# Function tables of the scalar engine, loaded by one-element activations placed ahead of waits

## The chip, the core and the metric

The kernel runs on one core of a Trainium2 chip. A core has five engines that run their own instruction streams and meet at semaphores: TensorE (matmul; PE in the profile, PEld its weight loads), VectorE (DVE), ScalarE (ACT), GpSimd (POOL) and SyncE (SP). Sixteen DMA engines move data between the device memory and the core's two on-chip memories. The metric is the device time of one execution in microseconds.

ScalarE computes functions such as Exp, Sqrt, Sigmoid, Silu and GELU from tables. The tables come in sets; an instruction ACT_TABLE_LOAD in its stream puts another set in place. The programmer doesn't write these loads: they are inserted into the program where an activation needs a table that isn't in place. Copy, Identity, Square and Relu need no set of their own.

## The reference, cut to what matters

A token block of 256 x 1024 goes through three parts. Part one (one layer):

```python
mod = silu(c) @ w_ada + b_ada                      # nine rows of modulation
h = modulate(rmsnorm(x), m0, m1); y = swiglu(h)    # ffn 1
x = x + 0.5 * m2 * rmsnorm(y)
h = modulate(rmsnorm(x), m3, m4)                   # sparse attention beside an LRU
x = x + m5 * rmsnorm(concat(rmsnorm(attn), rmsnorm(lru)) @ w_out)
h = modulate(rmsnorm(x), m6, m7); y = swiglu(h)    # ffn 2
x = x + 0.5 * m8 * rmsnorm(y)
```

Parts two and three are two layers of a second block. Each has a mixer (HGRN2, dilated attention and Mamba2 side by side, between two RMS norms) and a layer of picked experts: 8 heads pick 16 experts per token each, and for each pick `x += gelu(h . down[e]) * gate * up[e]`.

## The kernel before, in words

**Part one** goes stage by stage through both 128-token blocks. On ScalarE each RMS norm is a `mean_square`: a Square over the row with an accumulated sum, a wait for it, and a Sqrt of one element per partition. It is called by `pre` (norm of x, after a wait for `x_ready`), `post` (norm of a product in PSUM, after a wait for `tiles_used`) and `attn_norm` (after a wait for `attn_scaled`). The feed-forward gates are Silu (L1314, in `ffn`).

**Parts two and three** run over four units i = 0 to 3: two layers by two token blocks. Each has a mixer (`mixer_scalar`, `mixer_vector`, `mixer_tensor`) and then its picks (`picks_scalar`, `picks_vector`, `picks_tensor`, `picks_pool`). Mixer 0 runs alone (`lone`). Mixers 1 to 3 run beside the picks of the unit before: a mixer is a generator that yields a slot number ahead of each of its steps, and `Beside.to(slot)` runs all steps up to that slot. The picks of a unit are 8 heads x 8 rounds = 64 rounds of two picks; on ScalarE and VectorE round r calls `beside.to(2 * r + 1)`, so slots go up to 127, and on TensorE each of the 128 picks calls `beside.to(k)`. The order of the work on each engine is so written out by hand.

One round of picks: POOL gathers a pick's row of 2 x 1024 values (down and up) for each of 128 tokens (L1158), into a ring of 8 buffers; VectorE takes the dot product with h (L1107); ScalarE takes the GELU of two dots (L1021); VectorE multiplies by the gate (L1118); ScalarE scales the identity to two diagonal matrices (L1026); TensorE adds diagonal x up row into PSUM (L1040). POOL gathers into a buffer again when TensorE has used it (`ups_used`). VectorE waits for the GELU of a round before it goes on to the next round's dots.

Once a head, `exps(u + 1)` takes the exponentials of the next head's scores (L1007), at the start of a head; for the head that begins the next unit it is taken in the last head's third round. `opening` runs ahead of the first round of all: `post(2, 1)`, the last norm of part one, for the second token block.

The mixer's steps on ScalarE that need tables, with their slots: L316 Sqrt (1), L327 Sigmoid (13), L342 and L343 Exp (28), L362, L363 and L385 to L387 Silu (42; 50 for L362 and L363 when not lone), L396 Sqrt (46), L378 Sqrt (46 lone, else 55), L419 and L422 Exp (57), L429 Exp in `probs` (62 and 67), L367 Silu (55 lone, else 68), L446 Sqrt (69), L464 Sqrt (91). Steps that only copy lie between them.

The weights come over SP's queue in tiles of 1 MB into a ring of four buffers; TensorE frees one with `tiles_used`. The second feed-forward's down product of the second token block (L1753, "late" tiles) is spread through mixer 0 on TensorE and ends just ahead of `opening`.

Of the kernel before, what the change touches and what calls it, by code (L numbers as in the profile page):

```python
# [6 lines left out]


# [1 line left out]

# [1 line left out]

# [8 lines left out]
ACT = mybir.ActivationFunctionType  # L21
AX = mybir.AxisListType

P = 128
# [26 lines left out]
EXPERT_HEADS = 8  # L51
# [6 lines left out]
ROUNDS = K16 // ROUND  # L58
# [35 lines left out]
def columns(spec):  # L94

    at, out = 0, {}
    for name, n in spec:
        out[name] = at
        at += n
    return out, at  # L100
# [8 lines left out]
CONST = [("ident", P), ("eps", 1), ("iota", K16), ("ones", P), ("tri", P), ("trineg", P), ("hmask", 7 * P)]  # L109
EARLY = P + 1 + K16  # L110
WAVE = 3
CONST1 = [("t5", BANK), ("dil", BANK), ("chunk", TB * S)]
CC1, WC1 = columns(CONST1)
CC, WC = columns(CONST)


def program(nc, wts, ada, c_row, small1, small2, consts, consts1, x_in, lb_in, normrow, experts, out):
    ctx = ExitStack()
    with ctx:
        def sb(name, shape, dt=F32, stack=ctx):  # L120
            return stack.enter_context(nc.sbuf_tensor(name, shape, dt))

        def sem(name):
            return ctx.enter_context(nc.semaphore(name))
# [6 lines left out]
        bias_d1 = sb("bias_d1", [P, A2, S])  # L131
        stat = sb("stat", [P, 64])
        mst = sb("mst", [P, 72])
        s2 = sb("s2", [P, LAYERS, W2])
        lbt = sb("lbt", [P, 8])
        PS = ctx.enter_context(nc.psum_tensor("PS", [P, 8, BANK], F32))
# [26 lines left out]
        m = {n: sem(n) for n in names}  # L163
# [91 lines left out]
        def o1(name, a=0, n=1, rows=P):  # L255
            return s1[0:rows, C1[name] + a:C1[name] + a + n]
# [21 lines left out]
        class Count:  # L278
# [4 lines left out]
            def next(self):  # L283
                self.n += 1
                return self.n

        class Beside:
# [3 lines left out]
                self.at = next(steps, None)  # L291

            def to(self, slot):
                while self.at is not None and self.at <= slot:
                    self.at = next(self.steps, None)

        def mixer_scalar(act, i):
            lone = i == 0
# [5 lines left out]
                return PS[:, c % 2, :]  # L304

            yield 1
            if i >= TB:
                act.wait_ge(m["x_added"], i - TB + 1)
            else:
                act.wait_ge(m["x_ready"], 5 + i)  # L310
                act.wait_ge(m["smalls2_loaded"], 32)
# [53 lines left out]
            def chunk6():  # L365
                a = chunk(6)
                act.activation(u[:, 640:768], a[:, 0:128], ACT.Silu)  # L367
                act.copy(v_tok[:, tb, :], a[:, 128:512]).then_inc(m["u_copied"], 1)

            def o_squares():  # L370
                act.wait_ge(m["o_done"], i + 1)
                for h in range(4):
                    act.activation(osq[:, h * DH:(h + 1) * DH], PS[:, 1, h * DH:(h + 1) * DH], ACT.Square,
                                   accum_out=mst[:, 28 + h:29 + h]).then_inc(m["o_sq"], 1)

            def o_root():
                act.wait_ge(m["o_sq"], 4 * i + 4)
                act.activation(mst[:, 32:36], mst[:, 28:32], ACT.Sqrt, bias=C("eps"), scale=1.0 / DH).then_inc(m["o_root"], 1)  # L378
# [12 lines left out]
                act.copy(Wx.rearrange("p (b n) -> p b n", b=2), PS[:, G2:G2 + 2, 0:256]).then_inc(m["cross_copied"], 1)  # L391
            yield 46
            if lone:
                o_squares()
            act.wait_ge(m["qk_sums"], i + 1)
            act.activation(mst[:, 16:28], mst[:, 4:16], ACT.Sqrt, bias=C("eps"), scale=1.0 / DH).then_inc(m["qk_root"], 1)  # L396
# [17 lines left out]
            else:  # L414
                o_squares()
                o_root()
            yield 57
            act.wait_ge(m["cum_in"], i + 1)
            act.activation(dts[:, 78:90], dts[:, 66:78], ACT.Exp).then_inc(m["cum_exp"], 1)  # L419
            act.wait_ge(m["cum_T"], i + 1)  # L420
# [17 lines left out]
            if not lone:  # L438
                chunk6()
            yield 69  # L440
            act.wait_ge(m["y_gated"], i + 1)
            for g in range(2):
                act.activation(Wx[:, 192 * g:192 * g + 192], mx[:, 640 + 192 * g:832 + 192 * g], ACT.Square,
# [10 lines left out]
            for b in (0, 1):  # L454
# [3 lines left out]
                                          scale=o2(l, "mix_g", c))  # L458
                last.then_inc(m["hT_mix"], 1)
            yield 91  # L460
            act.wait_ge(m["x_out"], i + 1)
            act.activation(flat(lgt)[:, 0:D], x[:, tb, :], ACT.Square, accum_out=mst[:, 2:3]).then_inc(m["out_sq"], 1)
            act.wait_ge(m["out_sq"], i + 1)
# [539 lines left out]
        def picks_scalar(act, i, beside=None, opening=None):  # L1003

            def exps(u):
                act.wait_ge(m["topk_ready"], u + 1)
                act.activation(topf[:, 128 + 32 * (u % 2):144 + 32 * (u % 2)], topf[:, 112 + 32 * (u % 2):128 + 32 * (u % 2)],  # L1007
                               ACT.Exp).then_inc(m["gate_exp"], 1)

            if i == 0:  # L1010
                exps(0)
            for h in range(EXPERT_HEADS):
                u = EXPERT_HEADS * i + h
                if h + 1 < EXPERT_HEADS:
                    exps(u + 1)
                if u == 0:
                    opening()
                for rr in range(ROUNDS):
                    rnd = u * ROUNDS + rr
                    act.wait_ge(m["dots_done"], rnd * ROUND + ROUND)  # L1020
                    act.activation(coef[:, 0, rr % 2, :], dots[:, rr % 2, :], ACT.Gelu_apprx_tanh).then_inc(m["gelu_ready"], 1)  # L1021
                    act.wait_ge(m["coef_ready"], rnd + 1)
                    if rnd * ROUND >= RING:
                        act.wait_ge(m["ups_used"], rnd * ROUND + ROUND - RING)
                    for j in range(ROUND):
                        act.activation(diag[:, (rr * ROUND + j) % RING, :], ident, ACT.Copy, scale=coef[:, 1, rr % 2, j:j + 1])\  # L1026
                            .then_inc(m["diag_ready"], 1)
                    if beside:
                        beside.to(2 * (h * ROUNDS + rr) + 1)
                        if h + 1 == EXPERT_HEADS and rr == 2:  # L1030
                            exps(u + 1)

        def picks_tensor(pe, i, beside=None):
            if i:
                pe.wait_ge(m["x_added"], i)
            for k in range(PICKS):
                n = PICKS * i + k
                pe.wait_ge(m["diag_ready"], n + 1)
                for half in range(2):
                    last = pe.matmul(PS[:, ACC + half, :], diag[:, n % RING, :], ups[:, n % RING, half * BANK:(half + 1) * BANK],  # L1040
                                     start=k == 0, stop=k == PICKS - 1, skip_group_check=True)
                last.then_inc(m["ups_used"], 1)
                if beside:
                    beside.to(k)
# [142 lines left out]
        def _(sp):  # L1187
            for n in range(TILES):
# [4 lines left out]
                elif n == 2:  # L1193
                    sp.wait_ge(tile_loaded[0], 16)
                elif n == WAVE:
                    sp.wait_ge(m["mod_added"], 14)
# [37 lines left out]
        def _(act):  # L1234
# [7 lines left out]

            def pre(k, tb):
                if k:
                    act.wait_ge(m["x_ready"], 2 * (k - 1) + tb + 1)
                mean_square(x[:, tb, :], D, 4 * k + 2 * tb, D, "x_root")

            def post(i, tb, done, bank):
                act.wait_ge(m["tiles_used"], done)
                mean_square(flat(PS[:, bank:bank + 2, :]), D, 12 + 4 * i + 2 * tb, D, "y_root_fb",  # L1250
                            flat(lgt) if i == 2 and tb else junk)
# [16 lines left out]
            act.dma_start(cst[:, 0:EARLY], consts[:, 0:EARLY]).then_inc(m["consts_loaded"], 16)  # L1268
            act.dma_start(s1[:, :], small1).then_inc(m["smalls_loaded"], 16)
            act.dma_start(cst1[0:33, 0:2 * BANK], consts1[0:33, 0:2 * BANK]).then_inc(m["strip_loaded"], 16)  # L1270
            act.wait_ge(m["c_spread"], 1)
            act.activation(cact[:, :], flat(PS[:, 0:2, :]), ACT.Silu).then_inc(m["c_act"], 1)
            act.wait_ge(m["x_loaded"], 16)
            act.wait_ge(m["consts_loaded"], 16)
            for tb in range(TB):
                pre(0, tb)
# [139 lines left out]
                act.copy(dst, flat(PS[:, bank:bank + 2, :])).then_inc(m["probs_copied"], 1)  # L1416

            def attn_norm(tb):
                act.wait_ge(m["attn_scaled"], tb + 1)
                mean_square(attn[:, tb, :], D_ATTN, 24 + 2 * tb, D_ATTN, "attn_root")  # L1420

            def attn_evacuate(tb):
                act.wait_ge(m["attn_T"], tb + 1)
                for c in range(4):
                    last = act.activation(mT[:, c, tb * P:(tb + 1) * P], PS[:, 4 + tb, c * P:(c + 1) * P], ACT.Copy,
                                          scale=o1("attn_g", c))
                last.then_inc(m["attn_by_scalar"], 1)
# [16 lines left out]
            act.activation(scr1[:, 2048:3072], scr1[:, 0:1024], ACT.Square).then_inc(m["lru_sq"], 1)  # L1444
            attn_norm(1)
            attn_evacuate(1)
            act.wait_ge(m["lru_sumsq"], 1)
            act.activation(lroot, PS[:, 6, 0:S], ACT.Sqrt, bias=C("eps"), scale=1.0 / D_ATTN)\
                .then_inc(m["lru_root"], 1)
# [15 lines left out]
        def _(pe):  # L1465
# [60 lines left out]
            def gate_up(f):  # L1526
# [8 lines left out]

                for j in range(0 if f else WAVE, 4):
                    step(j, 0, True)
# [38 lines left out]
            for c in range(3, KC):  # L1576
                for j in range(WAVE):
                    wave(j, c, c + 1)
# [202 lines left out]
        def _(v):  # L1781
            V = Chain(v, m["chain_v"])
# [67 lines left out]
            def pair_columns(c):  # L1850
# [3 lines left out]
                v.scalar_tensor_tensor(prea[:, c:c + 1], modc[:, 8 + c:9 + c], 1.0, o1("pre_g", c), ALU.add, ALU.mult)\  # L1854
                    .then_inc(m["first_cols"], 1)

            v.memset(silu[0:1, 0, 0:P], 1.0).then_inc(m["c_ones"], 1)
            v.wait_ge(m["c_act"], 1)
            pair_sums(0)
# [289 lines left out]
```

## Time and profile before

| | us |
|---|---|
| Median of three runs | 2228.6 (2226.3 to 2235.58) |
| The profiled execution, whole | 2231.29 |
| Its span in the profile | 2229.6 |
| TensorE busy | 1983.0 (89%) |
| VectorE busy | 1293.3 (58%) |
| ScalarE busy | 631.8 (28%) |
| GpSimd busy | 610.2 (27%) |

The profile shows one execution. The span counts from its first to its last instruction; the execution lasts 1.7 us longer. A line such as L1021 is that line of the kernel. Registers, branches and the issue of DMAs do not count as busy. The mean granted clock of TensorE is 0.97 of full speed. A group of instructions has the idle time of its engine just before them, and what ended most of it. The chain that ended last is followed back from the last instruction to what released it.

### The profile page before, as it was taken

What the parts mean: (1) busy time and instruction counts of PE and PEld (TensorE: products, weight loads), DVE (VectorE), ACT (ScalarE), POOL (GpSimd) and SP (SyncE); (2) the same over time, 40 slices, a digit from 0 to 9 for tenths busy, and PEclk for the clock granted to TensorE, in tenths of its full rate; (3) what the DMA queues carried; (4) which work ended last, traced back from release to release, by engine and by line L of the source; (5) the groups of instructions that cost most, each with busy time, mean ns of one, the idle gap of its engine ahead of it and who ended that gap; (6) DMA issues with size and microseconds to landing.
All of it is one profiled execution on the core that took longest, in us unless ns stands there. A gap on an engine that the chain in (4) does not pass through costs nothing.

```text
span 2229.6 us, 20053 instructions
## 1 busy us (share of the span) xinstructions
PE 1983.0 (89%) x6132; PEld 1065.8 (48%) x6132; DVE 1293.3 (58%) x3375; ACT 631.8 (28%) x1517; POOL 610.2 (27%) x554
## 2 busy tenths in 40 slices
PE   7999999899999898888879998998989899777776
PEld 5885587588644344443434443443434444333322
DVE  5550254200033567786576877657687767777764
ACT  2000234200024222543142255223235422222221
POOL 1100000000000233443343333334334334454442
PEclk9999999999999999999999999999999999899999
DMA  9988834444676899999999999999999999999997
GB/s 394 421 351 310 313 114 150 170 151 151 243 266 222 323 420 421 413 419 400 421 413 421 421 420 402 403 422 412 421 406 410 391 420 406 399 421 422 421 421 320
DMA packets 113382, 793.89 MB, mean 356 GB/s; under 512 B 12378, under 2 KB 16090, under 8 KB 18442
## 3 DMA queue, kind: packets, MB, share of 16 engines
q0 software_dynamic: 78912, 574.65, 62.5%
q1 hardware_dynamic: 28944, 207.73, 24.7%
q10 hardware_dynamic: 5434, 10.41, 1.3%
q8 instruction: 42, 0.69, 0.1%
q14 instruction: 50, 0.41, 0.0%
HBM read 791.67 MB, written 4.75 MB: 357 GB/s over the span
## 4 chain that ended last, share of the span: by engine, by line
PE 54%; DMA 22%; DVE 12%; ACT 7%; issue 4%; POOL 1%; POOLq 0%; DVEq 0%; ACTq 0%
DMA wide<-experts_in,pick_idx 20%; PE PS L1474 16%; PE PS L1040 16%; PE PS L496 9%; PE PS L1548 6%; DVE wide L1107 4%; ACT diag L1026 2%; PE PS L1753 1%; ACT L1021 1%; POOL wide L1158 1%; DMA ring<-wts_in 1%; DMA early<-ada_in 1%; PE PS L1505 1%; DVE topi L1055 1%; DVE topi L1058 1%
## 5 line engine op out<-in xcount | busy, mean ns | idle before, releaser
L1040 PE MATMUL PS<-wide,diag 128*128 128x512 f32 x2048 | 988.6, 621 | 206.4 <-ACT diag L1026 197.1
L1158 POOL DMA_INDIRECT wide<-experts_in,pick_idx x512 | 582.8, 1138 | 1286.8 <-PE PS L1040 793.1
L1107 DVE CUSTOM_DVE_ANT_0 wide<-wide,htok 128x1024 f32<-128x1024 f32 x512 | 619.2, 1224 | 242.1 <-DMA wide<-experts_in,pick_idx 235.0
L1040 PEld LDWEIGHTS PS<-wide,diag 128*128 128x128 f32 x2048 | 386.5, 197 | 727.1 <-issue 419.7
L1474 PE MATMUL PS<-hT,ring 128*128 128x256 f32 x1648 | 360.4, 381 | 4.5 <-ACT hT L1257 1.9
L1474 PEld LDWEIGHTS PS<-hT,ring 128*128 128x128 f32 x1648 | 313.9, 191 | 50.5 <-issue 5.8
L496 PE MATMUL PS<-ring,hTm 128*128 128x512 f32 (+1 forms) x704 | 321.8, 586 | 1.9 <-ACT hTm L321 0.8
L1026 ACT ACTIVATE diag<-cst,coef 128x128 f32<-128x128 f32 x512 | 177.6, 394 | 271.9 <-DVE coef L1118 266.7
L1021 ACT ACTIVATE coef<-dots 128x2 f32<-128x2 f32 x256 | 52.1, 204 | 590.5 <-DVE dots L1107 589.9
L496 PEld LDWEIGHTS PS<-ring,hTm 128*128 128x128 f32 x704 | 133.0, 191 | 161.5 <-issue 153.2
L1548 PE MATMUL PS<-ring,actT 128*128 128x512 f32 x264 | 116.1, 600 | 2.4 <-DMA ring<-wts_in 2.4
L1818 DVE TENSOR_TENSOR actT<-silu,PS 128x256 f32<-128x256 f32 (+1 forms) x44 | 18.5, 420 | 170.5 <-ACT silu L1314 170.5
L1314 ACT ACTIVATE silu<-PS 128x256 f32<-128x256 f32 x44 | 16.9, 384 | 271.9 <-PE PS L1474 269.7
L1118 DVE TENSOR_TENSOR coef<-coef,gate 128x2 f32<-128x2 f32 x256 | 41.3, 161 | 87.1 <-ACT coef L1021 74.5
L1811 DVE CUSTOM_DVE_ANT_0 early<-early,cact 128x1024 f32<-128x1024 f32 x56 | 67.0, 1222 | 42.7 <-DMA early<-ada_in 42.7
L1548 PEld LDWEIGHTS PS<-ring,actT 128*128 128x128 f32 x264 | 50.4, 192 | 65.4 <-issue 61.4
L1021 ACT ACT_TABLE_LOAD x61 | 78.3, 1283 | 1.1
L1793 DVE RECIPROCAL stat<-stat 128x1 f32<-128x1 f32 x6 | 1.0, 164 | 111.9 <-ACT stat L1240 111.9
L1228 POOL TENSOR_TENSOR bias_t<-bias_t,early 128x1024 f32<-128x1024 f32 (+1 forms) x2 | 7.9, 3932 | 187.4 <-DVE early L1925 187.4
L1221 POOL DMA_DIRECT2D early<-ada_in x32 | 17.0, 530 | 107.6 <-DVE modr L1811 89.7
L1107 DVE DVE_READ_ACCUMULATOR2_ANT dots<- 128x1 f32 x512 | 42.1, 82 | 0.0
L1753 PE MATMUL PS<-ring,actT 128*128 128x512 f32 x88 | 38.9, 594 | 0.0
(337 smaller groups left out, 1363.4 us busy)
## 6 DMA issues: line engine op xcount, KB each, us to landing
ring<-wts_in SPq DMA_DIRECT2D x191, 1024.0 KB, 5.7
early<-ada_in POOLq DMA_DIRECT2D x36, 1024.0 KB, 12.8
wide<-experts_in,pick_idx POOLq DMA_INDIRECT x512, 11.8
ring<-wts_in SPq DMA_DIRECT2D x8, 780.0 KB, 8.5
strip_t<-strips_one ACTq DMA_DIRECT2D x1, 2048.0 KB, 11.5
strip_dil<-strips_one ACTq DMA_DIRECT2D x1, 1536.0 KB, 19.5
x<-x_in ACTq DMA_DIRECT2D x1, 1024.0 KB, 5.5
bias_t<-strip_t ACTq DMA_DIRECT2D x1, 1024.0 KB, 14.3
```

Of the source, the lines that this page charges most:

```text
L496: last = pe.matmul(PS[:, c % 2, 0:n], hTm[:, k, :], w[:, k % 4 * n:(k % 4 + 1) * n], start=k == 0, stop=k == 7, skip_group_check=True)
L1021: act.activation(coef[:, 0, rr % 2, :], dots[:, rr % 2, :], ACT.Gelu_apprx_tanh).then_inc(m["gelu_ready"], 1)
L1026: act.activation(diag[:, (rr * ROUND + j) % RING, :], ident, ACT.Copy, scale=coef[:, 1, rr % 2, j:j + 1])\
L1040: last = pe.matmul(PS[:, ACC + half, :], diag[:, n % RING, :], ups[:, n % RING, half * BANK:(half + 1) * BANK], start=k == 0, stop=k == PI ...
L1055: V(v.max_index(where[:, 0:8], vals[:, 0:8], row))
L1107: v.tensor_tensor_reduce(out=downs[:, n % RING, :], in0=downs[:, n % RING, :], in1=htok[:, tb, :], scale=1.0, scalar=0.0, op0=ALU.mult, op ...
L1118: v.tensor_tensor(coef[:, 1, rr % 2, :], coef[:, 0, rr % 2, :], gate[:, u % 4, rr * ROUND:(rr + 1) * ROUND], ALU.mult)\
L1158: pool.indirect_dma_start(pairs_of_rows[:, k % RING, :, :].rearrange("p c n -> p (c n)"), None, experts.rearrange("l e d -> (l e) d"), bas ...
L1474: last = pe.matmul(outp, a, b, start=i == 0, stop=i == len(pairs) - 1)
L1548: last = pe.matmul(PS[:, bank + half, :], src[:, 2 * t + k, tb * P:(tb + 1) * P], w[:, k * D + half * BANK:k * D + (half + 1) * BANK], sta ...
L1753: last = pe.matmul(PS[:, 6 + half, :], actT[:, 2 * t + k, P:S], w[:, k * D + half * BANK:k * D + (half + 1) * BANK], start=t == k == 0, st ...
L1811: v.tensor_tensor_reduce(out=w, in0=w, in1=cact[:, :], scale=1.0, scalar=0.0, op0=ALU.mult, op1=ALU.add, accum_out=modr[:, 8 * j + n:8 * j ...
```

## The change

A helper `warm(act, func)` issues a one-element activation (per partition) of a function, from a column of ones to one of 100 columns that nobody reads. Calls of it stand ahead of the waits of ScalarE's norms, of some steps of mixer 0, and in the picks: at the start of each head and at the end of each round in which a mixer step ran. `Beside.to` now says whether a step ran. A memset on VectorE at the very start writes the ones.

```diff
+        warmed = sb("warmed", [P, 1 + WARMED])
             def to(self, slot):
+                ran = False
                 while self.at is not None and self.at <= slot:
                     self.at = next(self.steps, None)
+                    ran = True
+                return ran
+
+        warm_at = itertools.count()
+
+        def warm(act, func):
+            c = next(warm_at) % WARMED + 1
+            act.activation(warmed[:, c:c + 1], warmed[:, 0:1], func)
...
 # mixer_scalar, each after its yield and ahead of the waits
             yield 1
+            if lone:
+                warm(act, ACT.Sqrt)
...
             yield 46
             if lone:
+                warm(act, ACT.Sqrt)
                 o_squares()
...
             yield 57
+            if lone:
+                warm(act, ACT.Exp)
...
             yield 69
+            if lone:
+                warm(act, ACT.Sqrt)
...
             yield 91
+            if lone:
+                warm(act, ACT.Sqrt)
...
 # picks_scalar
             if i == 0:
+                warm(act, ACT.Exp)
                 exps(0)
             for h in range(EXPERT_HEADS):
                 u = EXPERT_HEADS * i + h
                 if h + 1 < EXPERT_HEADS:
                     exps(u + 1)
                 if u == 0:
                     opening()
+                warm(act, ACT.Gelu_apprx_tanh)
                 for rr in range(ROUNDS):
...
                     if beside:
-                        beside.to(2 * (h * ROUNDS + rr) + 1)
+                        ran = beside.to(2 * (h * ROUNDS + rr) + 1)
                         if h + 1 == EXPERT_HEADS and rr == 2:
                             exps(u + 1)
+                        if ran or h + 1 == EXPERT_HEADS and rr == 2:
+                            warm(act, ACT.Gelu_apprx_tanh)
...
             def pre(k, tb):
                 if k:
+                    warm(act, ACT.Sqrt)
                     act.wait_ge(m["x_ready"], 2 * (k - 1) + tb + 1)
...
             def post(i, tb, done, bank):
+                warm(act, ACT.Sqrt)
                 act.wait_ge(m["tiles_used"], done)
...
+            act.wait_ge(m["c_ones"], 1)
             act.wait_ge(m["c_spread"], 1)
             act.activation(cact[:, :], flat(PS[:, 0:2, :]), ACT.Silu).then_inc(m["c_act"], 1)
+            warm(act, ACT.Sqrt)
             act.wait_ge(m["x_loaded"], 16)
...
             def attn_norm(tb):
+                warm(act, ACT.Sqrt)
                 act.wait_ge(m["attn_scaled"], tb + 1)
...
             attn_evacuate(1)
+            warm(act, ACT.Sqrt)
             act.wait_ge(m["lru_sumsq"], 1)
...
+            V(v.memset(warmed[:, 0:1], 1.0))
             v.memset(silu[0:1, 0, 0:P], 1.0).then_inc(m["c_ones"], 1)
```

## Rows read from the trace of the kernel before

**Rows 1.** The page, part 4: shares of the chain that ended last, by line.

```profile
DMA wide<-experts_in,pick_idx 20%; PE PS L1474 16%; PE PS L1040 16%; PE PS L496 9%; PE PS L1548 6%; DVE wide L1107 4%; ACT diag L1026 2%; PE PS L1753 1%; ACT L1021 1%; POOL wide L1158 1%; DMA ring<-wts_in 1%; DMA early<-ada_in 1%; PE PS L1505 1%; DVE topi L1055 1%; DVE topi L1058 1%
```

**Rows 2.** The page, part 5: groups; busy us, mean ns, idle before, releaser.

```profile
L1021 ACT ACTIVATE coef<-dots 128x2 f32<-128x2 f32 x256 | 52.1, 204 | 590.5 <-DVE dots L1107 589.9
...
L1021 ACT ACT_TABLE_LOAD x61 | 78.3, 1283 | 1.1
```

**Rows 3.** Timeline of ScalarE: start us, us, what, [idle before, releaser].

```profile
424.74 1.28 ACT L1314 ACT_TABLE_LOAD   x1
433.46 0.38 ACT L1314 ACTIVATE silu<-PS 128x256 f32<-128x256 f32 x1 [7.44 <-PE PS L1474]
```

**Rows 4.** The chain in order of time: start us, us, what; at the start and at 616.

```profile
9.35 12.54 DMA early<-ada_in
...
616.23 10.30 PE PS L1753 x24
```

**Rows 5.** Timeline of ScalarE, the square of attn_norm(0).

```profile
372.33 0.63 ACT L1238 ACTIVATE silu<-early 128x512 f32<-128x512 f32 x1 [0.33 <-DVE early L1965]
```

**Rows 6.** Timeline of all engines, 695 to 699, mixer 0.

```profile
695.77 0.36 ACT L443 ACTIVATE Wx<-mx 128x192 f32<-128x192 f32 x1 [1.52 <-DVE mx L978]
...
696.13 1.88 PE L1753 MATMUL PS<-ring,actT 128*128 128x512 f32 x4
...
698.71 1.10 PE L683 MATMUL PS<-v_tok,hTm 128*128 128x64 f32 x8 [0.69 <-ACT hTm L449]
```

**Rows 7.** Timeline at the opening; last, a stage: window, us, engines, PEclk, DMA share, GB/s.

```profile
760.30 1.02 ACT L1238 ACTIVATE lgt<-PS 128x1024 f32<-128x1024 f32 x1 [6.09 <-PE PS L1753]
...
761.43 1.28 ACT L1240 ACT_TABLE_LOAD   x1
...
762.73 0.29 ACT L1240 ACTIVATE stat<-stat,cst 128x1 f32<-128x1 f32 x1
...
763.05 0.16 DVE L1793 RECIPROCAL stat<-stat 128x1 f32<-128x1 f32 x1 [2.02 <-ACT stat L1240]
...
764.00:766.00 2.00, 0.00 (x0) 0.00 (x0) 1.93 (x4) 0.53 (x2) 0.50 (x1) 0.50 0.98 414
```

**Rows 8.** Timeline of ScalarE, two small activations in a row.

```profile
652.37 0.21 ACT L342 ACTIVATE dts<-s 128x6 f32<-128x6 f32 x1 [0.92 <-DVE dts L869]
652.48 0.19 ACT L343 ACTIVATE dts<-dts 128x6 f32<-128x6 f32 x1
```

**Rows 9.** Waits: who waited for whom, us in total, times, longest.

```profile
DVE coef L1118 <- ACT coef L1021: 74.5, 65, 5.7
```

**Rows 10.** Timeline of ScalarE around slot 47 and slot 63 of unit 0.

```profile
917.07 1.28 ACT L1007 ACT_TABLE_LOAD   x1
...
918.60 1.28 ACT L1021 ACT_TABLE_LOAD   x1
...
960.20 1.28 ACT L429 ACT_TABLE_LOAD   x1
...
963.48 0.20 ACT L1007 ACTIVATE topf<-topf 128x16 f32<-128x16 f32 x1
963.69 1.28 ACT L1021 ACT_TABLE_LOAD   x1
```

**Rows 11.** Stages of 20 us; the last two columns are DMA share and GB/s.

```profile
1000.00:1020.00 20.00, 15.42 (x38) 6.74 (x38) 14.68 (x36) 8.31 (x23) 6.44 (x7) 0.91 0.95 378
...
1760.00:1780.00 20.00, 14.50 (x37) 6.45 (x36) 15.20 (x37) 8.43 (x23) 7.41 (x7) 0.91 0.90 358
```

**Rows 12.** Timeline of GpSimd and VectorE: issues of two gathers and their dots.

```profile
993.89 1.03 POOL L1158 DMA_INDIRECT wide<-experts_in,pick_idx  x1 [2.56 <-PE PS L1040]
...
1003.75 1.23 DVE L1107 CUSTOM_DVE_ANT_0 wide<-wide,htok 128x1024 f32<-128x1024 f32 x1 [0.77 <-DMA wide<-experts_in,pick_idx]
...
1012.37 1.05 POOL L1158 DMA_INDIRECT wide<-experts_in,pick_idx  x1 [6.31 <-PE PS L1040]
...
1018.64 1.23 DVE L1107 CUSTOM_DVE_ANT_0 wide<-wide,htok 128x1024 f32<-128x1024 f32 x1 [1.18 <-DMA wide<-experts_in,pick_idx]
```

More of the change, by code:

```diff
@@ L9 @@
 from contextlib import ExitStack
+import itertools
 import numpy as np
@@ L111 @@
 WAVE = 3
+WARMED = 100
 CONST1 = [("t5", BANK), ("dil", BANK), ("chunk", TB * S)]
```

## The prediction

> **What bounds the kernel now.** I read the page's shares of the chain that ended last first, then ScalarE's groups by line, then the table loads one by one along ScalarE's timeline. By line the chain is gather DMAs (20%) and TensorE matmuls; ScalarE's lines have 2% and 1% [rows 1]. So ScalarE, though it stands in every link, is seldom what is late. The second view decides what the change can do: 61 table loads in front of the GELU of L1021 take 78.3 us, and the idle time ahead of all 61 is 1.1 us, while the GELUs behind them idle 590.5 us waiting for dot products [rows 2]. A load is therefore run as soon as ScalarE reaches it, ahead of the wait of the activation that needs it. A single case shows the same: the load of L1314 starts at 424.74, its activation at 433.46 after 7.44 us of waiting for TensorE [rows 3]. Wherever an activation with one wait is itself the one that needs the table, the load is already where the change wants it. What the change can move are the loads that stand between a sum of squares (which needs no table of its own) and the root after it: there the wait is ahead of the squares, and the load behind them.
>
> The stages: up to about 745 us the kernel is bound by weight DMAs and then by TensorE; from 750 on the gathers saturate the DMA engines (share 0.98 to 1.05 in nearly every slice), with one dip in each of the three token blocks that have a mixer beside them: 0.95 in the slice at 1000, 0.90 in that at 1760, the third between them [rows 11].
>
> **What the change removes: loads from behind squares.** Each is one load of 1.28 us [rows 2]; what follows is whether anything was late because of it.
> - Start (L1240, pre(0, 0)): the chain there is two transfers of the modulation weights until 9.35 + 12.54 = 21.89 [rows 4], long behind ScalarE's root. Gain 0. The new memset ahead of c_ones and the wait for it lie beside the same transfers: 0.
> - post(0, 0) at 224 and post(2, 0) at 616: TensorE carries the chain through with other tiles, in the second case L1753, 10.30 us without a pause [rows 4]. Gain 0.
> - attn_norm(0), attn_norm(1): the idle time before the squares is 0.33 us in the first [rows 5] and none in the second, so the load only changes places with them. 0.33 less about 0.11 for the extra activation, then the same in loss: 0.
> - Mixer 0, L396 at 681: TensorE has tiles of L496 to work on meanwhile and goes on to its next turn without a pause. Gain 0.
> - Mixer 0, L446 at 696.59: on the chain, L443 to the load to L449 to L683. Ahead of L443 ScalarE idles 1.52 us, which just covers the load (1.28) and an activation. But TensorE is on L1753 until 696.13 + 1.88 = 698.01 and starts L683 at 698.71 [rows 6]: when the load goes, L1753 is late next. Gain 698.71 - 698.01 = 0.7 us, not 1.28.
> - The opening of the picks, post(2, 1): square at 760.30 after 6.09 us idle, load at 761.43, and VectorE starts on its root at 763.05 [rows 7]. VectorE, the first weights and the first diagonals come 1.28 earlier. The DMA engines are at share 0.98 in the slice that follows [rows 7], so the freed buffers join a full queue. Between 0 and 1.28; I take 0.6, since the queue is full but the first re-issue comes late (POOL waits there).
> Sum: -1.3 us (bounds -2.0 and -0.7).
>
> **What it adds: activations.** Counting the code: 119 in the picks (one for each of 32 heads, one after each of 28 rounds in which a mixer step ran, one more in the last head, the last two in three blocks), and some 20 elsewhere that lie in waits. Behind another ready activation, a small one costs the spacing of L342 and L343, 0.11 us; at most its length of 0.19 [rows 8]. It costs nothing where ScalarE then waits for dot products. It counts where VectorE waits for the GELU, which the waits give 65 times [rows 9]: 65 x 0.11 = 7.2 us (upper bound 65 x 0.19 = 12.4).
>
> **What it adds: table loads.** This is the part that the words of the change do not mention. The diff puts a GELU activation at the end of every round in which a mixer step ran. In the last round of a head the next thing on ScalarE is not a GELU but the exponential of L1007. Two mixer steps with other tables fall on such rounds, at slots 47 and 63 of the 128:
> - Slot 47: L396 (root), then L1007's load at 917.07, then L1021's at 918.60 [rows 10]. With a GELU between L396 and L1007 there is one load more.
> - Slot 63: L429 (exponential) with its load at 960.20, then L1007 at 963.48 with none, as the table is there, then L1021's load at 963.69 [rows 10]. With a GELU between them, both a GELU load and an exponential load are added: two more.
> Three loads in each of three blocks: 9 x 1.283 = 11.5 us of ScalarE, always where VectorE sits waiting for the GELU. The Trainium skill, ScalarE: Activation LUTs, Rules for kernel authors, says to group calls by table set and to finish one set before switching; slot 63 is where the old code does so and the new code does not. By that rule the sum is the one just made.
>
> The waits that are added (c_ones) are met long before ScalarE comes there. Of the queues, none is passed: the activations stand ahead of waits and behind issued DMAs. Queued behind each extra load are the GELU, the two diagonals, TensorE's products and then POOL's next gather.
>
> **How much of it reaches the end.** ScalarE's extra time is 11.5 + 7.2 = 18.7 us, 6.2 in each of three blocks. A gather that is issued later need not land later as long as the DMA queue holds others. The gather of the pick dotted at 1003.75 was issued at 993.89, 9.9 us before; the one dotted at 1018.64 was issued at 1012.37, 6.3 us before, with the DMA engines just run dry [rows 12]. The difference, 3.6 us, is an estimate of what the queue can swallow ahead of the dip. So a block is longer by 6.2 - 3.6 = 2.6 us, three by 7.8 us. Bounds: 0, if a faster stretch behind the mixer's rounds gives it all back, and 18.7 if nothing is swallowed.
>
> Sum: -1.3 + 7.8 = +6.5 us. The profiled execution took 2231.3 (span 2229.6 and 1.7 around it) and would take 2237.8; the median of the runs is 2228.6, 2.7 lower, so I forecast 2228.6 + 6.5 = 2235 us.
>
> **Rivals.**
> 1. Nothing is swallowed. Between 910 and 990 VectorE hardly waits for gathers; the chain there runs through ScalarE and VectorE, and a longer link is then longer 1:1. For it: DMA share still dips in each block, so the ring of eight rows is empty once per block [rows 11]. Against it: the share is 1.01 throughout the very stretch in which the loads are added. Time 2228.6 - 1.3 + 18.7 = 2246.0. It decides once the added delay exceeds those 3.6 us by much in a single stretch. 21%.
> 2. All is swallowed, or the compiler adds no loads at the two slots. Only the gains show: 2228.6 - 2.0 = 2226.6, to 2228. For it: from 750 on bytes over rate set the pace. 23%.
> 3. The loads do not now run ahead of the waits, and the change takes the 61 off the chain: up to 61 x 1.28 = 78 us less, 2150. Against it: 1.1 us of idle time ahead of 61 loads [rows 2]. 1%. Some gain of over 11 us from elsewhere, for which I have no row: 3%.
> 4. A switch costs more than its load, up to twice as much. Then the nine cost 9 x 2 x 1.283 = 23.1 us, and the time is 2228.6 - 1.3 + 23.1 + 7.2 - 3 x 3.6 = 2246.8. Against it: the load ends at 761.43 + 1.28 = 762.71 and its activation starts at 762.73 [rows 7], so 1.28 is all. 3%. The Trainium skill, ScalarE: Activation LUTs, What ACT_TABLE_LOAD costs, does put a drain of about 1.38 us on every switch, 2.66 in all; the rows do not agree.
>
> **How the numbers follow.** Likeliest case 49%, 2231 to 2241 by the bounds of its terms; rivals 21, 23, 4 and 3%. The range 2226 to 2246 holds the likeliest, most of rival 2 and the lower part of rival 1. A measurement of this kernel tells about 0.5%, 11 us, from no change: slower is above 2239.7, faster below 2217.5. Slower: rivals 1 and 4 and an upper slice of the likeliest, 0.27. Faster: 0.04. Within: 0.69.
>
> **What would show it.** In ScalarE's groups, L1007's and L1021's loads, with those of the new activations, up by 9 from 89, and 6 loads of L1240 (now moved to the new line) no longer behind squares. At slot 63, four loads where two stood. The idle time of VectorE before L1118 up by 10 to 18 us. The first diagonal about 2 us earlier. DMA shares at the three dips lower by 0.1 each if the likeliest holds, unchanged in rival 2. I am wrong in the main step if the number of loads is not up, or if it is and the dips have not moved.

## The result and the profile after

| | before | changed |
|---|---|---|
| Median, us | 2228.6 (2224.02 to 2235.58, 7 runs) | 2244.49 (2239.87 to 2251.61, 7 runs) |
| Ratio | | 1.0076, 95% interval 1.0063 to 1.0088 |
| Span of the profiled execution, us | 2229.6 | 2247.4 |
| ScalarE busy, us | 631.8 | 658.9 |
| Mean granted clock of TensorE | 0.97 | 0.96 |

The changed kernel is slower: by 15.9 us between the medians, by 0.76% (17 us) in the ratio. The median is 1.5 us below the upper end of the stated range and 4.8 us above the 2239.7 us from which the forecast calls it slower. It is near the time of the first rival (2246) and 9.5 us above the likeliest case (2235).

In the changed kernel L308 is the new activation, L1029 is the old L1007 (exponentials of a head), L1045 the old L1021 (GELU), L1050 the old L1026 (diagonals), L1066 the old L1040, L1133 the old L1107 (dots), L1144 the old L1118, L1184 the old L1158 (gathers), L447 the old L429, L463 the old L443, L705 the old L683, L1785 the old L1753. Its groups, with busy us, mean ns and idle time before, answer [rows 2]:

```profile
L1045 ACT ACTIVATE coef<-dots 128x2 f32<-128x2 f32 x256 | 51.2, 200 | 569.9 <-DVE dots L1133 569.7
...
L308 ACT ACT_TABLE_LOAD x77 | 98.8, 1283 | 1.4
...
L1029 ACT ACT_TABLE_LOAD x30 | 38.5, 1283 | 0.4
L308 ACT ACTIVATE warmed<-warmed 128x1 f32<-128x1 f32 x139 | 28.1, 204 | 7.2 <-issue 6.4
```

The 61 loads of L1021 have moved to L308, with all the others that were moved; six more are new there, and three new ones stand at L1029, which lost one of its old loads to L308. Summed over all groups the loads went from 150 to 159. As before, a load waits for nothing (1.4 us ahead of 77), and the GELU behind it still idles 570 us.

Where the nine stand, on ScalarE's timeline of the changed kernel: slot 47 of unit 0 and slot 63 of unit 2. They answer [rows 10]:

```profile
919.55 1.28 ACT L308 ACT_TABLE_LOAD   x1
920.84 0.20 ACT L308 ACTIVATE warmed<-warmed 128x1 f32<-128x1 f32 x1
921.05 1.28 ACT L1029 ACT_TABLE_LOAD   x1
...
922.58 1.28 ACT L308 ACT_TABLE_LOAD   x1
...
1731.76 1.28 ACT L447 ACT_TABLE_LOAD   x1
...
1735.14 1.28 ACT L308 ACT_TABLE_LOAD   x1
...
1736.65 1.28 ACT L1029 ACT_TABLE_LOAD   x1
...
1738.17 1.28 ACT L308 ACT_TABLE_LOAD   x1
...
1739.58 0.19 ACT L1045 ACTIVATE coef<-dots 128x2 f32<-128x2 f32 x1
```

At slot 63 four loads stand where two stood: the exponential table is thrown out after 1735.14 and fetched again at 1736.65 for one activation of 0.22 us.

The gains ahead of the picks are there too. Timeline of all engines, mixer 0 (answers [rows 6]) and the opening (answers [rows 7]):

```profile
695.44 0.36 ACT L463 ACTIVATE Wx<-mx 128x192 f32<-128x192 f32 x1
...
695.80 1.88 PE L1785 MATMUL PS<-ring,actT 128*128 128x512 f32 x4
...
697.52 1.00 PE L705 MATMUL PS<-v_tok,hTm 128*128 128x64 f32 x8
...
759.01 1.02 ACT L1264 ACTIVATE lgt<-PS 128x1024 f32<-128x1024 f32 x1 [4.59 <-PE PS L1785]
...
760.48 0.16 DVE L1825 RECIPROCAL stat<-stat 128x1 f32<-128x1 f32 x1 [0.58 <-ACT stat L1266]
```

From the squares to TensorE's next product: 2.08 us, before 2.94, so 0.86 less (forecast 0.7; L1785 is what is late now). From the square of the opening to VectorE: 1.47 us, before 2.75, the one load of 1.28 less. The first diagonals start at 764.69 instead of 767.26, 2.6 us earlier.

### The profile page after: what moved, and what is told of

Read it like the earlier page. It is cut to its first block, busy times and chain, and to the rows that moved or that the text cites. A ratio compares the mean times of both kernels' runs of the same rounds, so it can differ in the third digit from the quotient of the medians.

```text
span 2247.4 us, 20203 instructions
## 1 busy us (share of the span) xinstructions
PE 2007.3 (89%) x6132; PEld 1080.2 (48%) x6132; DVE 1292.3 (58%) x3376; ACT 658.9 (29%) x1665; POOL 616.3 (27%) x554
## 4 chain that ended last, share of the span: by engine, by line
PE 59%; DMA 20%; DVE 9%; ACT 6%; issue 4%; POOL 1%; POOLq 0%; DVEq 0%; ACTq 0%
PE PS L1066 20%; DMA wide<-experts_in,pick_idx 18%; PE PS L1506 16%; PE PS L518 10%; PE PS L1580 6%; DVE wide L1133 3%; PE PS L1785 2%; ACT diag L1050 1%; ACT L308 1%; POOL wide L1184 1%; DMA ring<-wts_in 1%; DMA early<-ada_in 1%; PE PS L512 1%; PE PS L1537 1%; ACT L1029 1%
## 5 line engine op out<-in xcount | busy, mean ns | idle before, releaser
L1066 PE MATMUL PS<-wide,diag 128*128 128x512 f32 x2048 | 1005.1, 631 | 201.3 <-ACT diag L1050 195.2
L1184 POOL DMA_INDIRECT wide<-experts_in,pick_idx x512 | 589.0, 1150 | 1298.7 <-PE PS L1066 804.6
L1133 DVE CUSTOM_DVE_ANT_0 wide<-wide,htok 128x1024 f32<-128x1024 f32 x512 | 618.4, 1223 | 237.1 <-DMA wide<-experts_in,pick_idx 230.3
L1066 PEld LDWEIGHTS PS<-wide,diag 128*128 128x128 f32 x2048 | 393.0, 200 | 725.2 <-issue 429.0
L1050 ACT ACTIVATE diag<-cst,coef 128x128 f32<-128x128 f32 x512 | 177.6, 394 | 274.9 <-DVE coef L1144 274.9
L1045 ACT ACTIVATE coef<-dots 128x2 f32<-128x2 f32 x256 | 51.2, 200 | 569.9 <-DVE dots L1133 569.7
L1144 DVE TENSOR_TENSOR coef<-coef,gate 128x2 f32<-128x2 f32 x256 | 41.1, 161 | 118.9 <-ACT coef L1045 100.6
L1133 DVE DVE_READ_ACCUMULATOR2_ANT dots<- 128x1 f32 x512 | 41.8, 82 | 0.0
L1785 PE MATMUL PS<-ring,actT 128*128 128x512 f32 x88 | 38.9, 594 | 0.0
## 6 DMA issues: line engine op xcount, KB each, us to landing
strip_dil<-strips_one ACTq DMA_DIRECT2D x1, 1536.0 KB, 18.7
```

The lines of the kernel that those rows point to most:

```text
L1133: v.tensor_tensor_reduce(out=downs[:, n % RING, :], in0=downs[:, n % RING, :], in1=htok[:, tb, :], scale=1.0, scalar=0.0, op0=ALU.mult, op ...
L1144: v.tensor_tensor(coef[:, 1, rr % 2, :], coef[:, 0, rr % 2, :], gate[:, u % 4, rr * ROUND:(rr + 1) * ROUND], ALU.mult)\
L1184: pool.indirect_dma_start(pairs_of_rows[:, k % RING, :, :].rearrange("p c n -> p (c n)"), None, experts.rearrange("l e d -> (l e) d"), bas ...
L1785: last = pe.matmul(PS[:, 6 + half, :], actT[:, 2 * t + k, P:S], w[:, k * D + half * BANK:k * D + (half + 1) * BANK], start=t == k == 0, st ...
```

## The experiments

Two theories. L: what costs is the nine table loads at slots 47 and 63, on the chain of ScalarE. A: what costs is the 119 one-element activations. Each kernel was timed in five rounds beside the kernel before on the same chip; the ratios are to that, with 95% intervals.

**1. The nine loads alone.**

```diff
 # the kernel before, in picks_scalar, behind beside.to(...)
+                        if rr + 1 == ROUNDS and h in (2, 3):
+                            warm(act, ACT.Gelu_apprx_tanh)
```

> The kernel before with a GELU activation at the end of the last round of heads 2 and 3 of each unit with a mixer beside it, and nowhere else: 6 activations and the 9 table loads that they bring. Theory L (the loads on ScalarE's chain at slots 47 and 63 are the cost): 9 x 1.28 us reach the end nearly whole, 9 to 14 us over the kernel before, about 2240. Theory A (the 119 activations are the cost): 6 x 0.11, under 1 us over, 2229. My forecast of record (3.6 us of each block swallowed by the DMA queue): 3 x (4.1 - 3.6), under 3 us over.

Measured: 2242.96 us, ratio 1.0055 (1.0041 to 1.0068). The same kernel in a later series on another chip gave 2244.59 us, ratio 1.0050 (1.0032 to 1.0067), expected as

> The nine loads alone once more, on the same chip as the two kernels above: 0.55% again, within 0.14.

That is 11 to 12 us for 9 x 1.283 = 11.5 us of loads. Theory L holds, theory A falls for this part, and so does the forecast's term for what the queue swallows, which left under 3 us.

**2. The activations alone.** The same 119 places, with `ACT.Copy` in place of the GELU, and no front.

> The kernel before with all 119 activations of the picks, as copies, which need no table: activations without loads, and nothing changed ahead of the picks. Theory L: 0 to 4 us over the kernel before. Theory A: 8 to 17 us over.

Measured: 2232.62 us, ratio 1.0008 (0.9998 to 1.0018), 1.8 us. VectorE's wait for the GELU grew nonetheless, from the 74.5 us of [rows 9] to:

```profile
DVE coef L1134 <- ACT coef L1035: 83.0, 66, 5.8
```

8.5 us more of waiting, 7.2 by the forecast's reckoning, but some 2 us of it reach the end (at most 4.0 by the interval).

**3. The changed kernel without the 12 activations at head ends.**

```diff
-                        if ran or h + 1 == EXPERT_HEADS and rr == 2:
+                        if ran and (rr + 1 < ROUNDS or h + 1 == EXPERT_HEADS) or h + 1 == EXPERT_HEADS and rr == 2:
                             warm(act, ACT.Gelu_apprx_tanh)
```

> The changed kernel without the 12 activations that end the last round of a head where a mixer step ran and the next head's exponentials come next. It has the gains ahead of the picks, 107 activations in the picks, and 150 table loads as before. Theory L: -3 to +4 us against the kernel before. Theory A: +8 to +15, nearly as the changed kernel.

Measured: 2230.71 us, ratio 0.9991 (0.9978 to 1.0005). The whole loss is gone with 12 of 139 activations and the nine loads that they brought. The loads are 150 again, and at slot 63 the head's exponential runs on the mixer's table:

```profile
965.55 0.20 ACT L1029 ACTIVATE topf<-topf 128x16 f32<-128x16 f32 x1
965.76 1.28 ACT L308 ACT_TABLE_LOAD   x1
```

**4. The front alone** (no GELU activation in the picks).

> The changed kernel without any GELU activation in the picks: only the loads moved from behind squares, and the exponential at the first head. Both theories: -0.7 to -2.0 us against the kernel before, by the terms of the forecast; the square of post(2, 1) to the first diagonal shorter by one load. If the shift of the picks' start against the weights is itself harmful (a third theory), it is slower, by 2 us or more.

Measured: 2229.58 us, ratio 0.9992 (0.9980 to 1.0003): 1.8 us less, in keeping with the forecast's 1.3, but not told from no change.

**5. The changed kernel again.**

> The changed kernel as it is, beside the next three on one chip. If the parts add up (nine loads +0.55%, the activations +0.08%, the front -0.08%) it is 0.5 to 0.65% slower than before; if they make each other worse, 0.75 to 0.9%.

Measured: 2249.43 us, ratio 1.0082 (1.0068 to 1.0095). That is the second case: all parts together cost more than their sum. Experiment 8 asks which part does it.

**6 and 7. Three of the loads, and the other six.** `h == 2` alone (slot 47), then `h == 3` alone (slot 63).

> The kernel before with the GELU activation only at slot 47 of units 0 to 2: three loads of the nine, one in each block, 1.4 us each. If the queue swallows 3.6 us ahead of each dip, as the forecast has it: 0. If a load on the chain costs its length: 4 to 5 us. If the cost is one of place (a threshold that the two slots pass together): under 2 us here, and the rest at slot 63.

Measured: 2235.41 us, ratio 1.0023 (1.0011 to 1.0035).

> The kernel before with the GELU activation only at slot 63 of units 0 to 2: six loads, two in each block. By the price per load of the three loads at slot 47 (0.23%, 1.7 us each): 10 us, 0.46%. If parts add up to the nine loads' 0.55%: 0.32%, 7 us, 1.2 us a load.

Measured: 2237.89 us, ratio 1.0029 (1.0019 to 1.0039). 5.1 and 6.5 us; together 0.52%, the nine loads' 0.50 to 0.55%. A single load in a block already costs something near its length: 1.7 us each, 0.8 to 2.6 by the interval, against 1.28 and the activation's 0.2. There is no threshold of 3.6 us below which it is free. The six at slot 63 came out at 1.1 us a load, so a second load at one place was not seen to be dearer than the first.

**8. All activations and loads of the picks, without the front.**

> The changed kernel without anything ahead of the picks: all 119 GELU activations and the nine loads, on the front of the kernel before. If parts add up, nine loads (0.55%) and the copies (0.08%) give 0.63%. If the activations make the loads dearer, since they stand in the same stretches, 0.8 to 0.95%. If it was the front that made them dearer, 0.55 to 0.65% here and the rest is in the changed front.

Measured: 2245.92 us, ratio 1.0064 (1.0048 to 1.0079). Within the picks the parts add up: 0.55 + 0.08 = 0.63. By the third case of the expectation the rest of the changed kernel's loss comes with its front, which alone costs nothing; how isn't shown (see the end of the account below).

**9. Ten loads where ScalarE waits.**

```diff
 # the kernel before, in picks_scalar, behind the diagonals
+                    if i == MIXERS - 1 and rr == 6 and h in (1, 2, 3, 4, 5):
+                        warm(act, ACT.Sqrt)
```

> The kernel before with a square root activation behind the diagonals of round 6 of heads 1 to 5 of unit 3, where ScalarE then waits 3.54 us for dot products: five activations and ten loads (a root's and a GELU's each), 2.8 us at each place. Theory of place: the loads fit into the wait, 0 to 1 us in all. If every load costs its length wherever it stands: 12.8 us.

Measured: 2230.65 us, ratio 0.9999 (0.9989 to 1.0009), 0.2 us less, with an interval of 2.5 us less to 2.0 us more. More loads than the changed kernel adds, at no cost that can be told from none. ScalarE's timeline shows why, one of the five places:

```profile
1974.75 1.28 ACT L308 ACT_TABLE_LOAD   x1
...
1976.25 1.28 ACT L1034 ACT_TABLE_LOAD   x1
1978.26 0.20 ACT L1034 ACTIVATE coef<-dots 128x2 f32<-128x2 f32 x1 [0.72 <-DVE dots L1122]
```

The GELU still waits 0.72 us for its dots behind both loads, and 0.72 to 0.74 us in the other four places. So the price is one of place.

**10. Moving loads out of the head starts.**

```diff
+                late = h not in (0, 4)
-                if h + 1 < EXPERT_HEADS:
+                if h + 1 < EXPERT_HEADS and not late:
                     exps(u + 1)
...
+                    if late and rr == 0 and h + 1 < EXPERT_HEADS:
+                        exps(u + 1)
                     if beside:
```

> The kernel before with the exponentials of the next head taken behind the diagonals of the head's first round instead of ahead of its first GELU, but for heads 0 and 4. The same activations and at most one load more in each block; at some 20 head starts an exponential load, its activation and the GELU's load (2.8 us) leave the place where the GELU is late for one where ScalarE waits 2 to 6 us. Theory of place: faster, -4 to -12 us, less if the gathers' 31 us of idle DMA is not reached by it. If the number of loads alone counts: 0.

Measured: 2234.43 us, ratio 1.0018 (1.0006 to 1.0030), slower. The expectation was wrong. In heads 5 and 6 of the units with a mixer the exponentials now stand ahead of the mixer's evacuation (L457) that TensorE waits for: TensorE's wait for it at this place is 4.65 us, before 3.09. ScalarE's timeline and a stage of 20 us (last columns: granted clock, DMA share, GB/s):

```profile
1006.24 1.28 ACT L1007 ACT_TABLE_LOAD   x1
...
1007.65 2.15 ACT L457 ACTIVATE hTm<-PS,s 128x128 f32<-128x128 f32 x8
1009.83 1.28 ACT L1022 ACT_TABLE_LOAD   x1
...
1000.00:1020.00 20.00, 14.03 (x31) 6.43 (x32) 12.85 (x30) 8.23 (x22) 5.28 (x6) 0.83 0.84 332
```

The dip that was 0.95 in [rows 11] is 0.84 here.

**11. The same in heads 1 to 3 only** (and 4 to 6 of unit 3).

> The kernel before with the next head's exponentials behind the first round's diagonals in heads 1, 2 and 3 of every unit and in heads 4 to 6 of unit 3, but no longer in heads 5 and 6 of the units with a mixer, where they stood ahead of the mixer's evacuations (slots 81 and 97) and cost 2 to 3 us each in the trace of the former try. Theory of place: -2 to -7 us. If moving the loads gains nothing anywhere: 0 to +3.

Measured: 2230.14 us, ratio 0.9991 (0.9979 to 1.0003). The dip at 1000 is 0.96 again and VectorE waits less for the GELU than before:

```profile
DVE coef L1121 <- ACT coef L1022: 62.3, 55, 5.4
...
1000.00:1020.00 20.00, 16.16 (x39) 7.45 (x40) 13.89 (x34) 9.13 (x25) 8.26 (x6) 0.91 0.96 380
```

12 us less waiting, and a gain of 2.0 us that can't be told from none; the expected gain began at 2. With the 8.5 us of experiment 2 this says the same twice: this wait, summed over the picks, is not the price. No kernel of the study beats the kernel before beyond its interval.

## Why a load at slot 63 costs what it does

I follow one place. TensorE's timeline and stages of 2 us around slot 63 of unit 0, in the kernel before (stage columns as in [rows 7]):

```profile
965.93 1.98 PE L1040 MATMUL PS<-wide,diag 128*128 128x512 f32 x4 [1.65 <-ACT diag L1026]
...
966.00:968.00 2.00, 2.00 (x7) 1.04 (x8) 1.97 (x6) 0.17 (x1) 0.00 (x0) 1.00 0.99 414
```

and in the changed kernel:

```profile
973.28 3.78 PE L1066 MATMUL PS<-wide,diag 128*128 128x512 f32 x4 [4.67 <-ACT diag L1050]
...
970.00:972.00 2.00, 0.00 (x0) 0.00 (x0) 0.00 (x0) 1.97 (x3) 0.00 (x0) 0.79 1.05 438
...
974.00:976.00 2.00, 2.00 (x3) 0.67 (x2) 2.00 (x5) 0.00 (x0) 0.00 (x0) 0.50 1.01 422
976.00:978.00 2.00, 2.00 (x8) 1.48 (x7) 1.93 (x4) 0.68 (x3) 0.12 (x1) 0.50 0.44 180
978.00:980.00 2.00, 2.00 (x14) 1.76 (x14) 1.97 (x6) 1.97 (x4) 1.44 (x1) 1.00 0.00 0
```

TensorE has nothing else to do there and waits for the diagonals: 1.65 us before, 4.67 us in the changed kernel, 3.0 more for two loads and two activations. After 1.65 us idle its granted clock is still 1.00. In the longer pause it falls to 0.50, the lower of the two levels (0.79 as the mean of the stage from 970 to 972, 0.50 from 974), and the four matmuls behind it take 3.78 us instead of 1.98: another 1.8 us. GpSimd's issues of the gathers show the sum, first in the kernel before:

```profile
964.45 0.94 POOL L1158 DMA_INDIRECT wide<-experts_in,pick_idx  x1 [0.57 <-issue]
968.72 1.31 POOL L1158 DMA_INDIRECT wide<-experts_in,pick_idx  x1 [3.33 <-PE PS L1040]
```

and in the changed kernel:

```profile
968.79 0.94 POOL L1184 DMA_INDIRECT wide<-experts_in,pick_idx  x1 [0.66 <-issue]
977.88 1.56 POOL L1184 DMA_INDIRECT wide<-experts_in,pick_idx  x1 [8.15 <-PE PS L1066]
```

4.3 us between two issues, then 9.1: 4.8 longer, which is 3.0 + 1.8. The queue runs dry at 977 and stays so until 980. By the two stages that is (1.01 - 0.44) x 2 + 1.01 x 2 = 3.2 us, so on the side of the gathers some 1.6 of the 4.8 us is swallowed.

VectorE shows why that does not make the loads cheaper. Its dots on either side of slot 63 and the wait between them, in the kernel before:

```profile
959.37 1.22 DVE L1107 CUSTOM_DVE_ANT_0 wide<-wide,htok 128x1024 f32<-128x1024 f32 x1
...
965.28 0.16 DVE L1118 TENSOR_TENSOR coef<-coef,gate 128x2 f32<-128x2 f32 x1 [2.21 <-ACT coef L1021]
...
966.25 1.22 DVE L1107 CUSTOM_DVE_ANT_0 wide<-wide,htok 128x1024 f32<-128x1024 f32 x1
```

and in the changed kernel:

```profile
963.71 1.22 DVE L1133 CUSTOM_DVE_ANT_0 wide<-wide,htok 128x1024 f32<-128x1024 f32 x1
...
972.63 0.16 DVE L1144 TENSOR_TENSOR coef<-coef,gate 128x2 f32<-128x2 f32 x1 [5.32 <-ACT coef L1045]
...
973.60 1.22 DVE L1133 CUSTOM_DVE_ANT_0 wide<-wide,htok 128x1024 f32<-128x1024 f32 x1
```

The changed kernel's dots are 4.34 us behind the old ones ahead of slot 63 and 7.35 us behind them after it, 3.0 more at once. VectorE waits here for the GELU, and its dots for no gather: in the kernel before none of them does between 938 and 992. A full queue of gathers can't swallow a delay of an engine that is waiting for something else. Followed on through the same block, the dots stay 7.4 to 8.6 us behind until the old dip, and are 6.4 us behind after it (1034.42 against 1028.05). So slot 63 costs this block 2.0 us.

What the lower clock adds differs from run to run. In the changed kernel it is back at 1.00 by 978, and the dots fall behind by another 0.5 us. In the kernel with the six loads it stayed at 0.50 until 976, and the mixer's product (L509, the old L496) is late by it. The kernel before, then that kernel (L380 is the old L367):

```profile
973.17 1.88 PE L496 MATMUL PS<-ring,hTm 128*128 128x512 f32 x4
...
977.02 0.28 ACT L367 ACTIVATE u<-PS 128x128 f32<-128x128 f32 x1
```

```profile
966.90 3.78 PE L1055 MATMUL PS<-wide,diag 128*128 128x512 f32 x4 [4.58 <-ACT diag L1039]
...
978.80 1.88 PE L509 MATMUL PS<-ring,hTm 128*128 128x512 f32 x4
...
980.72 0.28 ACT L380 ACTIVATE u<-PS 128x128 f32<-128x128 f32 x1 [2.74 <-PE PS L509]
```

TensorE is 0.97 us behind the kernel before at 966.90 and 5.63 us behind at 978.80. ScalarE, which stands ahead of a GELU there, waits 2.74 us for it, and VectorE's dots fall from 1.0 to 3.7 us behind.

The dips of [rows 11] move too; stages of the changed kernel:

```profile
960.00:980.00 20.00, 14.16 (x42) 7.24 (x41) 14.27 (x39) 12.16 (x27) 6.75 (x5) 0.83 0.85 357
1000.00:1020.00 20.00, 16.61 (x47) 8.13 (x47) 16.07 (x40) 8.62 (x25) 6.72 (x7) 0.91 1.01 421
...
1740.00:1760.00 20.00, 19.50 (x53) 11.20 (x54) 13.55 (x36) 13.17 (x30) 6.31 (x5) 0.77 0.74 283
```

and of the kernel with the six loads of slot 63 alone:

```profile
960.00:980.00 20.00, 15.42 (x39) 8.56 (x38) 12.39 (x30) 13.52 (x29) 4.79 (x5) 0.74 0.72 276
```

The old dip at 1000 is gone (1.01), a deeper one stands right behind slot 63. Part of each delay is so paid back at the old dip, and the mean price of slot 63 per block is 2.2 us (6.5 us in three blocks) instead of the 3.2 us of idle DMA. That the fall of the clock makes part of the price is read from these rows of three executions. It wasn't tried apart, since no kernel here kept TensorE busy through the pause.

## Why the prediction was right or wrong, point by point

The direction and the nine loads were right, the likeliest case was not. It had 6.5 us of loss, 15.9 were measured, and the time lies in the stated range only because that range took in the lower part of the first rival. That rival has the mechanism that the runs show: ahead of the dip VectorE waits for ScalarE and hardly for gathers, and a longer link is then longer 1:1. Its number is in part luck: of its 18.7 us the activations were 7.2 and cost 1.8 alone, and 4 to 5 us of the measured loss belong to no part that was tried alone.

- **That a load already runs ahead of the wait of its own activation.** Right. The GELU's 61 loads gave nothing by being issued through another activation: without the 12 at head ends (experiment 3) the kernel can't be told from the kernel before.
- **The front, -1.3 us.** Right in size in the trace (0.86 and 1.28 at the two places); 0.08% less in the timing, within noise.
- **Nine more loads, at slots 47 and 63, and at no other place.** Right: 150 to 159, and taking away the activations that bring them takes away the loss.
- **The activations, 65 x 0.11 = 7.2 us.** VectorE's wait is up by 8.5 us, but 1.8 us reach the end (-0.4 to 4.0), so the term was 5.4 us too large. Which of the activations those are wasn't tried.
- **3.6 us swallowed in each block.** This is the step that failed. The forecast took 10.8 us off both terms together; in the runs the loads alone pay 11 to 12 us of 11.5. Two reasons are seen. The 3.6 us came from the rows of the old dip, where both dots do wait for their gathers (0.77 and 1.18 us in [rows 12]). It was laid against delays at slots 47 and 63, 30 us and more earlier, and at slot 63 VectorE waits for the GELU and for no gather: the dots are 3.0 us later at once, and only 1.3 us come back at the dip. And the delay was taken at its length, whereas TensorE's lower clock behind the longer pause makes the gathers' issue 1.8 us later still; in the two kernels looked at, VectorE fell behind by another 0.5 and 2.7 us.
- **What would show it.** Loads up by nine: yes. Four loads where two stood: yes. First diagonal about 2 us earlier: 2.6. VectorE's wait up by 10 to 18 us: up by 26. Its line in the changed kernel and in the kernel with the nine loads alone, against [rows 9]:

```profile
DVE coef L1144 <- ACT coef L1045: 100.6, 67, 6.4
...
DVE coef L1133 <- ACT coef L1034: 103.0, 67, 6.5
```

The nine loads alone raise it by 28.5 us and the time by 12, so this sum does not measure the delay. The dips were to be deeper by 0.1: they moved and are deeper by up to 0.16. None of these signs tested how much the queue swallows; they would have come out alike with nothing swallowed.
- **Rival 4 (a switch that costs twice its load).** Not borne out: 11 to 12 us for nine. The Trainium skill, ScalarE: Activation LUTs, What ACT_TABLE_LOAD costs, has a drain of 1.38 us on every switch. An estimate by that figure is 9 x 2.66 = 24 us. The trace doesn't agree: the ten loads of experiment 9, in waits of 3.54 us for each pair, would not have fitted at 2 x 2.66, and they did.
- **The rule against the change** (the Trainium skill, ScalarE: Activation LUTs, Rules for kernel authors: finish one table set before switching) is what the runs bear out, at slot 63 alone with 6.5 us.

Open: the changed kernel is 0.76 and 0.82% slower in two series, its picks without the front 0.64%, and the front alone 0.08% faster. Put together that is 0.56%, so 0.2 to 0.26%, some 5 us, have no cause shown. The intervals of the difference reach to zero or nearly, so I can't say whether front and picks make each other worse. The profiles give a hint and no more. From the first GELU to the 24th, a stretch that ends ahead of slot 47 and of every added load, the kernel before took 146.8 us and the changed kernel 151.4 and 151.1; the picks without the front and the nine loads alone took 149.0. The front alone took 150.7 there, the changed kernel without head ends 149.2, and kernels that changed nothing in this stretch 146.5 to 149.2.

## What to carry to other kernels

Before a table is fetched early, look where its load stands now: if the activation with the wait is the one that needs the table, the load already runs ahead of the wait, and an extra activation can only add. The loads worth moving are those behind an activation that needs no table; here they gave 0.86 and 1.28 us in the trace, too little to be told from none in the time. And follow the engine's order across the place where a helper is called: an activation set as a precaution at the end of a round put the wrong table in, because the next call was a different function, and nine loads at two tight places cost 11 to 12 us, while ten loads in waits cost nothing that could be measured. Before a queue is credited with swallowing a delay, look at the delayed place for what the next engine waits for: if it isn't the queue, the delay passes whole.

## What the runs showed of the hardware that I had not expected

- A pause of 1.65 us left TensorE's granted clock at 1.00, one of 4.67 us did not: four matmuls of 128x512 behind it took 3.78 us instead of 1.98. One of 3.09 us at the old dip of the kernel before (TensorE waits for L457 until 1008.27) did not either: the clock is 0.50 from 1010 to 1012. A delay of another engine can so cost more than its length where TensorE waits for it alone.
- VectorE's summed wait for ScalarE moved by +8.5 us (copies) and -12 us (exponentials in heads 1 to 3) with hardly any change of the time. A summed wait ranks places badly. The dips in the DMA share did better for the larger losses: 0.74 in the changed kernel, 0.72 with the six loads and 0.84 in experiment 10, where the kernel before has none under 0.90 beside its mixers. With the three loads of slot 47 (0.23%) the sign is small, 0.93 from 920 to 940 instead of 1.00, and kernels whose time didn't change have single slices as low (0.91 and 0.88 from 1520 to 1540 in experiments 9 and 11).
